# Third layer of a three-layer kernel: one block for group norm and both attentions, gate tiles moved into it, and the first expert written out ahead of the loop

## What is computed

```python
h = rms_norm_3(x, norm_mix_g)
na_q, na_k, na_v, p_r, p_k, p_v, lat_w, lat_a, lat_g, mem_q, gate_na, gate_rw, gate_mem = split_columns(h @ w_in)
y_na = neighborhood_attention(...)      # 6 heads of 64, bias from a table
y_rw = rwkv7_bidirectional(...)         # ends in a group norm, a bonus and a gate
y_mem = memory_attention(mem_q, rms_norm_3(mem, norm_mem_g), w_mem_kv)   # 4 heads, 256 memory rows
merged = sigmoid(gate_na) * (y_na @ w_branch_na) + sigmoid(gate_rw) * (y_rw @ w_branch_rw) + sigmoid(gate_mem) * (y_mem @ w_branch_mem)
x = x + merged @ w_out
# experts: 16, each takes its 32 best tokens (softmax of h @ w_router, top_k per expert)
act = silu(xe @ w_gate) * (xe @ w_up)   # 1024 -> 2048
ye = (act @ w_down) * top_val           # 2048 -> 1024, added back at the tokens' rows
return rms_norm_3(x, norm_final_g)
```

## Time and profile before

| what | value |
|---|---|
| median of 3 runs | 2255.42 us (2253.89 to 2257.35) |
| the profiled execution | 2251.1 us, its span 2249.3 us |
| TensorE busy | 1755.1 us (78%), mean granted clock 0.893 |
| VectorE, ScalarE, GpSimd busy | 405.5, 302.8, 19.2 us |
| HBM read | 555.90 MB |

### The profile page before, as it was taken

The page is one execution under the profiler, slowest core; times in us unless marked ns, Lnnn a source line. Parts: engine busy times, 40 slices in busy tenths (PEclk is TensorE's granted clock), DMA queues, the critical chain, the costliest instruction groups (busy, mean ns, idle before and its releaser), DMA issues. The chain is left out here.

```text
span 2249.3 us, 25422 instructions
## 1 busy us (share of the span) xinstructions
PE 1755.1 (78%) x11046; PEld 1050.1 (47%) x11046; DVE 405.5 (18%) x707; ACT 302.8 (13%) x482; POOL 19.2 (1%) x41
## 2 busy tenths in 40 slices
PE   3999999999999999999689785665655565666564
PEld 1866875887688558878467431111111111111111
DVE  0324522232100010446534300000000000000001
ACT  1140303241100010221211110000000000000001
POOL 0000000000000000000000000000000000000000
PEclk9999999999999999999868888888888878787876
DMA  9332370334644124410316269999999999999996
GB/s 344 108 129 76 113 253 16 136 132 154 219 150 149 66 95 159 150 39 3 55 40 265 108 288 429 429 428 428 429 428 429 429 428 429 428 429 428 428 429 251
DMA packets 119701, 558.04 MB, mean 248 GB/s; under 512 B 15496, under 2 KB 50253, under 8 KB 94925
## 3 DMA queue, kind: packets, MB, share of 16 engines
q1 hardware_dynamic: 115493, 545.61, 60.8%
q10 hardware_dynamic: 4136, 11.36, 1.3%
HBM read 555.90 MB, written 1.05 MB: 248 GB/s over the span
## 5 line engine op out<-in xcount | busy, mean ns | idle before, releaser
L3160 PE MATMUL ps<-ring,xn 128*32 128x512 f32 x2048 | 319.9, 757 | 215.9 <-DMA ring<-in_w_exp_up 114.4
L479 PE MATMUL ps<-hT,ring 128*128 128x256 f32 x1360 | 302.6, 385 | 4.5 <-DMA ring<-in_w_mem_kv 2.5
L479 PEld LDWEIGHTS ps<-hT,ring 128*128 128x128 f32 x1360 | 262.8, 194 | 43.6 <-issue 3.9
L3160 PEld LDWEIGHTS ps<-ring,xn 128*32 128x32 f32 x2048 | 63.2, 124 | 462.6 <-DMA ring<-in_w_exp_up 162.6
L3176 PE MATMUL ps<-ring,hT 128*32 128x512 f32 x1024 | 174.1, 814 | 111.7 <-DMA ring<-in_w_exp_down 104.1
L2218 PE MATMUL ps<-hT,ring 128*128 128x256 f32 x704 | 154.4, 383 | 2.0 <-PEq L838 1.9
L2218 PEld LDWEIGHTS ps<-hT,ring 128*128 128x128 f32 x704 | 135.1, 192 | 21.3 <-issue 2.8
L3176 PEld LDWEIGHTS ps<-ring,hT 128*32 128x32 f32 x1024 | 32.5, 131 | 235.6 <-DMA ring<-in_w_exp_down 174.9
L3204 DVE TENSOR_TENSOR hT<-hT,ps 128x512 f32<-128x512 f32 x16 | 11.0, 687 | 602.9 <-PE ps L3160 602.9
L1131 PE MATMUL ps<-hT,ring 128*128 128x256 f32 x512 | 119.5, 384 | 0.0
L1131 PEld LDWEIGHTS ps<-hT,ring 128*128 128x128 f32 x512 | 94.1, 190 | 13.2 <-issue 1.0
(11 more groups left out here) (530 smaller groups left out, 1398.2 us busy)
## 6 DMA issues: line engine op xcount, KB each, us to landing
ring<-in_w_exp_up SPq DMA_DIRECT2D x64, 2048.0 KB, 26.7
ring<-in_w_exp_gate SPq DMA_DIRECT2D x64, 2048.0 KB, 25.7
...
```

What stands on the lines that cost most here:

```text
L479: last = nc.tensor.matmul(k.ps[:, 2 * slot + n // 2, (n % 2) * S:(n % 2 + 1) * S], wt[:, c, n * P:(n + 1) * P], hT[:, c, 0:S], start=c == ...
L3160: last = nc.tensor.matmul(k.ps[32 * j:32 * j + 32, bank, :], xe[:, 2 * n + cc, :], slot(q, EFF)[:, cc, j * TILE:(j + 1) * TILE], start=n = ...
```

## The change

- Projection of the third layer: order is now three recurrence tiles, the 512 tile, query, key, memory keys, memory values, and two gate tiles; four gate tiles leave it. `mem` is loaded at its start, normed and turned inside it. The NA query is scaled in its copy.
- Last block of `rwkv`: SP loads the first of the four gate tiles and the 16 bias pieces after product step 3, and GpSimd adds the window mask to the (unmirrored) bias, two `tensor_tensor` of 128x1536, both inputs in SBUF.
- `group_norm_and_attentions` takes the place of blocks (3) to (5): eight attention units (four of 3 heads, four of 2), the sums of directions, the group norm and three turns, all on PSUM banks 4 to 7; the bias is added in PSUM by a second product per head; the 128 gate products stand between the steps.
- `third_merge`: branches on slots 2, 0, 3, output on slots 1, 4, whose loads are issued at the block's start; the second merge's semaphores are used again.
- Experts: the block of gather and spread is gone. The expert block begins with a small gather for expert 0 alone (16 products of 32 columns), and expert 0 is written out, with one chunk of the full gather behind each of its eight gate and up tiles, the turn of `weighted` behind them and two spreads behind each down tile. `weighted` moves behind the first tokens.
- Second layer: branch 1's weights share slot 2, branch 0's go to the slot of the third gate tile of the fill.

```diff
-    def __init__(self, k, name, branches, w_out):
+    def __init__(self, k, name, branches, w_out, slots=(0, 1, 2, 3, 4), earlier=None):
...
-            br["slot"], br["before"] = n, k.claim(n)
+            slot = slots[n]
+            at = slot * SLOT + br.get("at", 0)
+            br["weights"] = k.ring[:, at:at + br["chunks"] * D].rearrange("p (c n) -> p c n", n=D)
+            br["slot"], br["before"] = slot, None if "landed" in br else k.claim(slot)
+            self.loads.append((slot, br["before"], br["weights"], br["w"].rearrange("(c p) n -> p c n", p=P)))
-            slot = len(branches) + half
+            slot = slots[len(branches) + half]
...
             if p == 0:
-                pe.wait_ge(k.w_landed[br["slot"]], 16 * (br["before"] + 1))
+                if "landed" in br:
+                    pe.wait_ge(br["landed"], 16)
+                else:
+                    pe.wait_ge(k.w_landed[br["slot"]], 16 * (br["before"] + 1))
...
@@ third_merge
         @block.sync
         def _(sp):
+            issue(k, sp, m.loads[3:])
             issue(k, sp, ahead)
...
@@ GateFill
-    def __init__(self, k, name, tiles):
+    def __init__(self, k, name, tiles, first_slot=None):
         self.tiles, self.loads = [], []
+        if first_slot is not None:
+            k.next_slot = first_slot
         for w, gate in tiles:
@@ memory_and_sticks
         def _(sp):
-            issue(k, sp, ahead[0:1])
+            issue(k, sp, m.loads[2:3])
+            sp.dma_start(*m.loads[1][2:]).then_inc(m.branches[1]["landed"], 16)
             issue(k, sp, fill.loads[2:])
-            issue(k, sp, ahead[1:])
+            issue(k, sp, m.loads[0:1])
...
@@ second_layer
+                             "gate": k.gates(3, n), **({"at": 2 * D, "landed": k.sem("second_b_landed")} if n == 1 else {})} for n, name in enumerate(names)],
+              k.ins["w_o_2"][0], slots=(fill.tiles[2][0], 2, 2, 3, 4))
+    k.merge = m
+    memory_and_sticks(k, s, fill, k.xn, k.chan[:, 4:8, PAD:PAD + S], m)
@@ RwkvScratch
         self.lat_g = k.ring[:, at:at + S]
-        self.y, self.bonus = self.X, self.U
+        self.y, self.bonus = self.U, self.ak
+        self.bias = [k.ring[:, n:n + NA_H * S].rearrange("p (h n) -> p h n", h=NA_H) for n in (first + 4 * n6, first + 6 * n6)]
...
@@ rwkv_inputs
+    mem, mem_t = k.xs, mem_rows(k)
...
+        sp.dma_start(mem[:, :, :], k.ins["mem_3"].rearrange("b (t p) d -> p (b t) d", p=P)).then_inc(mem_landed, 16)
...
+    def memory_sums(act):
+        act.wait_ge(mem_landed, 16)
+        for t in range(TT):
+            last = nc.scalar.activation(mem_t[:, 4 * t:4 * t + 4, :].rearrange("p c s -> p (c s)"), mem[:, t, :], ACT.Square, accum_out=mem_sums[:, t:t + 1])
...
+    def turn_memory(pe):
+        pe.wait_ge(mem_normed, TT)
...
+    def copy_memory(act):
...
-    between = {4: {"scalar": latent},
-               5: {"tensor": low_rank(slice(0, 64), 0), "scalar": sigmoids(w_log, "rw_w0_3", 0)},
-               6: {"tensor": low_rank(slice(64, 128), 1), "scalar": sigmoids(b, "rw_a0_3", 1)},
-               7: {"tensor": sums, "scalar": decays}}
+    between = {0: {"scalar": memory_sums},
+               1: {"tensor": turn_memory, "scalar": copy_memory},
+               2: {"scalar": latent},
+               3: {"tensor": low_rank(slice(0, 64), 0), "scalar": sigmoids(w_log, "rw_w0_3", 0)},
+               4: {"tensor": low_rank(slice(64, 128), 1), "scalar": sigmoids(b, "rw_a0_3", 1)},
+               6: {"tensor": sums, "scalar": decays}}
...
@@ rwkv
-def rwkv(k, s, out, mem, bias):
+def rwkv(k, s, fill, out):
...
+        @block.sync
+        def _(sp):
+            sp.wait_ge(k.products, p0 + 3)
+            issue(k, sp, fill.loads[0:1])
+            load_bias(k, sp, s.bias, s.bias_landed)
+        @block.gpsimd
+        def _(pool):
+            pool.wait_ge(s.bias_landed, 16 * (S // GRID) ** 2)
+            for t in range(TT):
+                tile = s.bias[t].rearrange("p h (r c) -> p (h r) c", c=GRID)
+                nc.gpsimd.tensor_tensor(tile, tile, over(k.const("mirrored_window"), NA_H * S // GRID), ALU.add).then_inc(s.bias_ready, 1)
...
+def group_norm_and_attentions(k, s, fill, out, branch_loads):
...
+            sp.dma_start(gain, k.ins["rw_ln_g_3"].partition_broadcast(P).rearrange("p a n -> p (a n)")).then_inc(gains_landed, 16)
+            sp.dma_start(offset, k.ins["rw_ln_b_3"].partition_broadcast(P).rearrange("p a n -> p (a n)")).then_inc(gains_landed, 16)
+            sp.wait_ge(rows_summed, 2)
+            issue(k, sp, fill.loads[1:2])
+            issue(k, sp, (branch_loads[0], branch_loads[2]))
+            issue(k, sp, fill.loads[2:4])
+            issue(k, sp, branch_loads[1:2])
...
+            def spend(n):
+                for _ in range(n):
+                    next(more, None)
...
+            sum_rows(1, bonus)
+            sum_rows(0, y)
+            spend(6)
+            score(0)
+            score(1)
+            spend(12)
+            turn_probs(0)
+            spend(6)
+            turn_probs(1)
+            spend(4)
+            mix(0)
+            spend(2)
+            mix(1)
+            spend(8)
...
+            spend(8)
+            score(4)
+            score(5)
+            spend(8)
+            pe.wait_ge(rw_done, 1)
+            turn_y(y_rw, 3)
+            turn_probs(4)
+            spend(5)
...
+            spend(5)
+            pe.wait_ge(y_copied, 2)
+            pe.wait_ge(finished, 2 * LOCAL)
+            turn_y(y_mem, 2)
+            spend(1000)
...
+            exponential(0)
+            exponential(1)
+            fill.copy(k, act, 0)
+            copy(0)
+            act.wait_ge(squared, 1)
+            nc.scalar.activation(rstd, rstd, ACT.Sqrt, bias=k.const("gn_eps"), scale=1.0 / 64).then_inc(root, 1)
+            copy(1)
+            fill.copy(k, act, 1)
+            exponential(2)
...
+            exponential(6)
+            exponential(7)
+            fill.copy(k, act, 5)
+            copy(6)
+            copy(7)
+            fill.copy(k, act, 6)
+            fill.copy(k, act, 7)
...
@@ expert_choice
     k.advance(products=2, vectors=3, activations=1)
-    p0, v0, a0 = k.starts()
...
+            pool.wait_ge(spread_even, 1)
             nc.gpsimd.tensor_copy(way, back[:, 0, :]).then_inc(way_ready, 1)
+            pool.wait_ge(gathered_even, DC // 2)
+            pool.wait_ge(gathered_odd, DC // 2)
+            pool.wait_ge(spread_even, DC // 2)
+            pool.wait_ge(spread_odd, DC // 2)
...
-            pe.wait_ge(zeroed, 1)
-            for b in range(4):
-                nc.tensor.matmul(k.ps[:, b, :], zeros[:, 0:P], zeros, start=True, stop=True, skip_group_check=True)
+            for c in range(DC):
+                for t in range(TT):
+                    last = nc.tensor.matmul(k.ps[:, 0, c * CAP:(c + 1) * CAP], k.xs[:, t, c::DC], one_hot[:, t, 0:CAP], start=t == 0, stop=t == TT - 1)
+            last.then_inc(first_gathered, 1)
...
+            def gather(c):
+                if c == 3:
+                    pe.wait_ge(xe_ready, 1)
+                if c >= 4:
+                    pe.wait_ge((gathered_even, gathered_odd)[c % 2], (c - 4) // 2 + 1)
+                for t in range(TT):
+                    last = nc.tensor.matmul(k.ps[:, (c + 1) % 4, :], k.xs[:, t, c::DC], one_hot[:, t, :], start=t == 0, stop=t == TT - 1)
+                last.then_inc(gathered, 1)
...
+            def turn_weights():
+                pe.wait_ge(weights_ready, 1)
+                pe.wait_ge(gathered_even, DC // 2)
+                pe.wait_ge(gathered_odd, DC // 2)
...
+            def spread_ways(n):
+                if n == 0:
+                    pe.wait_ge(weights_copied, 1)
+                if n >= 4:
+                    pe.wait_ge((spread_even, spread_odd)[n % 2], (n - 4) // 2 + 1)
+                for e in (2 * n, 2 * n + 1):
+                    last = nc.tensor.matmul(k.ps[:, n % 4, e % 2 * S:(e % 2 + 1) * S], k.const(f"four_times{e % 4}"), turned_w[:, e // 4, :], start=True, stop=True)
...
+            def clear_sums():
+                pe.wait_ge(spread_even, DC // 2)
+                pe.wait_ge(spread_odd, DC // 2)
+                pe.wait_ge(zeroed, 1)
+                for b in range(4):
+                    nc.tensor.matmul(k.ps[:, b, :], zeros[:, 0:P], zeros, start=True, stop=True, skip_group_check=True)
...
-            with pe.Fori(0, EXP) as e:
+            def expert(e, opening):
                 pe.wait_ge(xe_ready, e + 1)
...
                         last.then_inc(k.tile_done[q % RING], 1)
+                        if opening:
+                            gather(q)
+                if opening:
+                    turn_weights()
                 pe.wait_ge(hidden, e + 2)
...
                     last.then_inc(k.tile_done[q % RING], 1)
+                    if opening:
+                        spread_ways(2 * j)
+                        spread_ways(2 * j + 1)
+                if opening:
+                    clear_sums()
...
```

(47 more changed lines are left out.)

625 lines of the change are left out of this document (318 added, 307 removed).

## The result

The changed kernel takes 2183.34 us, median of 4 runs (2182.44 to 2184.89); the kernel before took 2254.65 us beside it, median of 4 (2251.23 to 2257.35). The ratio is 0.968, 95% interval 0.967 to 0.970: 71.3 us faster by the medians. The forecast was 2178 us, 77.5 less. The medians differ by more, since the profiled execution of the kernel before, 2251.1 us, lies 3.5 under its median and that of the kernel after, 2182.44, only 0.9 under.

The account below looks back on a forecast made before the run. Expert-tile transfers (186 at 4.91 us) bind behind the first refill, so only time ahead of it counts. -39.6 - 10.0 - 3.1 - 3.4 - 22.4 + 1.0 = -77.5 us: profiled 2251.1 becomes 2173.6, median 2255.4 becomes 2178; range 2169 to 2196.

Parts of the forecast that it names:

- (a): Whole kernel: the parts come as summed, 2178 us, own range 2171 to 2188; chance 0.66.
- (b): Recurrence's end: GpSimd's two adds hold VectorE, 4 to 9.6 us on the path, 2182 to 2188; chance 0.12.
- Part 1: Third layer's projection: four gate tiles leave, memory keys, values and turn enter, TensorE stays the bound; -39.6 us.
- Part 2: Block of attentions: TensorE's work fills 91.5 us instead of 101.5, without stalls at full clock; -10.0 us.
- 64 records of 256 columns, 13.9: Block of attentions: TensorE's scores, 24 products for local heads and 8 for memory, take 13.9 us.
- Part 3: Third merge's first round: TensorE comes warm from the fill, 5.34 us instead of 8.43; -3.1 us.
- Part 4: Second layer: earlier load of w_out_lru removes TensorE's wait, so the next block starts earlier; -3.4 us.
- Part 5: Experts: `one_hot` to first refill takes 10.0 us instead of 32.4, first gather 6.0; -22.4 us, between 25.4 and 19.6 earlier.
- Part 6: Recurrence's last steps: bias loads land in time, GpSimd's window additions charged +1.0 us, between 0 and 9.6.
- (c): First expert: TensorE at half clock starves the load queue, 2.1 us lost per tile, 17 us, 2195; chance 0.10.
- (d): Block of attentions: the steps bind, a 2 us stall at each of ten waits, 20 us, 2198; chance 0.08.
- (e): Block of attentions: fill doesn't hold TensorE's clock, 180 us at half clock, slower than before, 2268; chance 0.03.

Follow-up runs that it names:

- e3: Kernel after with each local unit's bias products (512 and 256 columns) put ahead of its three 64-row score products: 2178.67 us.
- e7: Kernel after with the second layer's load of w_out_lru held back until the fourth gate tile is done: 2188.44 us.
- e9: Kernel after with unread 512-column products (one, five and two) where TensorE waits in the choice of tokens: 2182.16 us.
- e12: Kernel after with window added by VectorE, bias products first, unread products in the choice, and ScalarE laying the first gather's columns side by side: 2173.21 us.
- e10: Kernel after with GpSimd's two window additions moved behind the recurrence, into the start of the block of attentions: 2180.62 us.

## Why the prediction was right, and where its terms were off

The forecast, 2178, was 5.3 us low, and 2183.3 lies in the ranges of two of its cases: (a), the parts as summed, and (b), in which GpSimd's additions hold VectorE. The mechanism of (b) did occur, on top of parts that came mostly as described. Against the profiled executions, in which the parts were summed, the error is 8.9 us, -68.6 for -77.5. The median is nearer by luck: the forecast added to its sum the 4.3 us by which the profiled execution of the kernel before lay under the median it had then, and the kernel after's lay only 0.9 under. By its parts, predicted and measured in the profiled executions:

- **Part 1, -39.6: -39.7.** From the projection's first record to the recurrence's start 122.97 us instead of 162.67, VectorE's last record ends at 944.53, 9.6 us ahead of TensorE's last gate record (954.12), where I had worked out some 9.
- **Part 2, -10.0: -7.3.** No stall, clock 1.00. The failed term is "64 records of 256 columns, 13.9": the 48 of the local heads take 15.05 us alone, at 0.313 instead of 0.217, most of it because 64-row and 128-row products alternate (e3); the 16 of the memory take 2.1.
- **Part 3, -3.1: -2.1 in this trace**, 77.12 against 79.25, and -3.0 in the traces with 76.2. The first round starts warm; what the profiled execution gave back is one turn of rows at half clock.
- **Part 4, -3.4: -4.9.** The wait was priced right (3.5 in e7). Left out was the same term that part 3 has: a merge that starts warm, its 96 branch records 20.96 us instead of 22.43.
- **Part 5, -22.4: -19.9**, just inside my pessimistic end of 19.6. The failed step is the nearest row: I took the router's products, whose loads read neighbouring columns, for a gather that reads every eighth, and let the clock decide between 3.7 and 7.1. Measured 7.79, above the upper bound, and independent of the clock (e9, e12). The first tile took 3.64 against 2.8.
- **Part 6, +1.0: +5.6.** Some 4 us are the additions (3.7 against e10 and e12). The other 1.5 are the longer stretch at half clock in step 2, before any addition, which no part of the sum had and whose cause isn't known. The failed step is the price "1.0, between 0 and 9.6": rival (b) had the mechanism, the instruction and a size of 4 to 9.6, and came true with its lower end. The rule weighed there (the Trainium skill, "SBUF — State Buffer", "Who interferes with whom", by which a VectorE instruction with two SBUF inputs waits for GpSimd's reads) agrees with these traces: 2.74 us against 0.56, and no stretch of the instruction that reads PSUM. I gave it 0.12 since most of the steps' VectorE instructions read PSUM; one on the path was enough.

Together -39.7 - 7.3 - 2.1 - 4.9 - 19.9 + 5.6 = -68.3, against -68.6 by the spans. Rival (c) had its premise, the half clock at the first tile, but not its effect: the clock was up by the second, and the cadence stayed at 3.9 us. Rivals (d) and (e) did not occur: TensorE was busy for 93.3 of the 94.3 us of the block of attentions, at a clock of 1.00. The sum was safe because its large terms (39.6, 22.4) came from counted records, and no error was larger than part 6's 4.6; but apart from part 4's -1.5 and part 1, right to 0.1, they went the same way, which is how they came to some 9 us.
